# The start of a one-core transformer kernel: smaller first weight pieces, the first norm's squares added by GpSimd, and gates computed one block later

## The reference

```python
def rms_norm(x, g):
    xf = x.astype(jnp.float32)
    y = xf * lax.rsqrt(jnp.mean(xf * xf, axis=-1, keepdims=True) + EPS)
    return (y * g.astype(jnp.float32)).astype(x.dtype)

def even_mix(h, w_in, conv_w, conv_b, ln_g, ln_b, gate_w2, gate_b, gla_norm_g, w_out):
    ...
    p = h @ w_in
    ...
    a_val, a_gate, q, k, v, r, glr = jnp.split(p, cuts, axis=-1)
    y_a = conformer_conv(a_val, a_gate, conv_w, conv_b, ln_g, ln_b)
    log_a = jax.nn.log_sigmoid((glr @ gate_w2 + gate_b).astype(f32)) / GLA_GATE_TAU
    o = gla_chunked(q..., k..., v..., log_a...)
    o = rms_norm(o, gla_norm_g).reshape(B, S, hv).astype(h.dtype)
    y_b = o * jax.nn.silu(r)
    return jnp.concatenate([y_a, y_b], axis=-1) @ w_out

def first_block(x, ...):
    for layer in range(DEPTH):
        h = rms_norm(x, ev_norm_mix[j])
        x = x + even_mix(h, ...)
        h = rms_norm(x, ffn_norm[layer])
        x = x + peer_ffn(h, ...)
```

## Time and profile before

| | us |
|---|---|
| median of 3 runs | 2277.54 (2275.99 to 2280.52) |
| profiled execution | 2274.92, span 2273.1 |
| TensorE busy | 2242.3 (99%) |
| VectorE busy | 1743.5 (77%) |
| ScalarE busy | 1323.0 (58%) |
| GpSimd busy | 586.3 (26%) |

### The profile page before, as it was taken

How to read it: one execution, slowest core, us unless ns; L and a number is a source line. 1 busy time by engine, 2 the same in 40 slices (tenths; PEclk the granted TensorE clock), 3 DMA queues, 4 the chain that set the end, 5 groups by cost and what they waited for, 6 DMA issues and landing times.

```text
span 2273.1 us, 36462 instructions
## 1 busy us (share of the span) xinstructions
PE 2242.3 (99%) x13873; PEld 1964.5 (86%) x13873; DVE 1743.5 (77%) x3559; ACT 1323.0 (58%) x2400; POOL 586.3 (26%) x411
## 2 busy tenths in 40 slices
PE   8999999999999999999999999999999999999999
PEld 8889888888787878888988888888888878899998
DVE  7966999899787878667499998976666666747864
ACT  6765665665545554566566666555554455676643
POOL 4820388774000000011017887700000000003000
PEclk9999999999999999999999999999999999999999
DMA  7724577776788888665257777766666665324441
GB/s 275 254 96 146 187 191 185 173 169 168 267 295 282 292 285 292 256 213 202 93 183 193 190 176 171 169 215 223 216 220 217 216 242 205 130 112 176 185 192 61
DMA packets 168790, 455.24 MB, mean 200 GB/s; under 512 B 44885, under 2 KB 80285, under 8 KB 160681
## 3 DMA queue, kind: packets, MB, share of 16 engines
q1 hardware_dynamic: 135024, 452.40, 58.5%
q0 software_dynamic: 33280, 0.15, 4.1%
q10 hardware_dynamic: 312, 0.37, 0.1%
HBM read 432.76 MB, written 20.09 MB: 199 GB/s over the span
## 4 chain that ended last, share of the span: by engine, by line
PE 85%; DVE 9%; ACT 3%; DMA 2%; issue 1%; ACTq 0%; DVEq 0%
PE PS L174 85%; DVE r_sl L195 3%; DMA mem<-in_v 2%; DVE mem L195 2%; ACT r_sh L185 1%; DVE mem L203 1%; ACT mem L185 1%; DVE mem L209 1%; PE PS L177 0%; DVE hT L203 0%; ACT small L185 0%; DVE mem L215 0%; DMA mem<-in_ada 0%; DMA cst<-in_cst 0%; DVE r_gl L203 0%
## 5 line engine op out<-in xcount | busy, mean ns | idle before, releaser
L195 DVE TENSOR_TENSOR r_sl<-mem,r_sh 128x1024 fp32r<-128x1024 f32 (+2 forms) x750 | 896.3, 1196 | 375.6 <-ACT r_sh L185 374.3
L185 ACT ACTIVATE r_sh<-mem 128x1024 fp32r<-128x1024 f32 (+2 forms) x750 | 768.0, 1025 | 492.5 <-PE PS L174 394.7
L174 PE MATMUL PS<-r_h,r_sh 128*128 128x512 f32 (+2 forms) x3536 | 736.4, 350 | 8.9 <-ACT r_sh L185 4.0
L174 PEld LDWEIGHTS PS<-r_h,r_sh 128*128 128x128 f32 (+1 forms) x3536 | 559.7, 189 | 86.1 <-issue 8.5
L235 POOL DMA_INDIRECT gd<-mem x224 | 407.6, 1820 | 120.1 <-issue 77.5
L174 PEld LDWEIGHTS PS<-r_h,r_sl 128*128 128x128 f32 (+1 forms) x2832 | 381.0, 191 | 23.4 <-DVE r_sl L195 3.6
L174 PE MATMUL PS<-r_h,r_sl 128*128 128x256 f32 (+1 forms) x2832 | 399.7, 283 | 1.2 <-DVE r_sl L195 1.1
L174 PE MATMUL PS<-r_sh,r_ch 128*128 128x512 f32 x1024 | 277.1, 391 | 4.5 <-ACT r_sh L185 2.3
L174 PE MATMUL PS<-r_sh,r_cl 128*128 128x512 f32 x1024 | 274.8, 389 | 0.0
L174 PE MATMUL PS<-r_sl,r_ch 128*128 128x512 f32 x1024 | 274.7, 389 | 0.0
L174 PEld LDWEIGHTS PS<-r_sh,r_ch 128*128 128x128 f32 x1024 | 190.6, 188 | 51.7 <-ACT r_sh L185 7.5
(11 more groups left out here) (177 smaller groups left out, 2548.1 us busy)
## 6 DMA issues: line engine op xcount, KB each, us to landing
mem<-in_u SPq DMA_DIRECT2D x256, 512.0 KB, 3.9
mem<-in_v SPq DMA_DIRECT2D x256, 512.0 KB, 4.4
mem<-in_w SPq DMA_DIRECT2D x16, 2048.0 KB, 7.7
mem<-in_ada SPq DMA_DIRECT2D x48, 512.0 KB, 5.3
mem<-in_in SPq DMA_DIRECT2D x9, 2048.0 KB, 8.8
gd<-cst SPq DMA_DIRECT2D x16, 1024.0 KB, 9.8
mem<-in_wq SPq DMA_DIRECT2D x8, 2048.0 KB, 8.9
r_h<-gd SPq DMA_DIRECT2D x62, 256.0 KB, 4.8
```

Source lines behind the costliest of these rows:

```text
L174: return self.did(self.e and self.e.matmul(out, lhsT, rhs, start=start, stop=stop, skip_group_check=skip))
L185: return self.did(self.e and self.e.activation(out, in_, func, **kw))
L195: return self.did(self.e and self.e.tensor_tensor(out, a, b, op))
```

## The change

The second piece of the first projection's weights (512 columns) becomes three, of 128, 128 and 256 columns; SyncE starts the first four pieces at once, and the pieces behind them take other buffers of the ring. The squares of chunks 4 to 7 are made by VectorE, ahead of its first `gained_lo`; GpSimd adds the eight squares up, and a single product with ones stands between the high and the low matmuls of block 1. The gate products move behind block 2 and `turn_scale` behind block 3; on ScalarE the cuts of blocks 2 and 4 are moved ahead of the norm's scale and of the gates.

```diff
-EV_RANGES = [(2560, 2576), (1024, 1536), (512, 1024), (0, 512), (1536, 2048), (2048, 2560)]
+EV_RANGES = [(2560, 2576), (1024, 1152), (1152, 1280), (1280, 1536), (512, 1024), (0, 512), (1536, 2048), (2048, 2560)]
...
     def even_po(po):
...
-        for c in range(4, 8):
-            po.wait_ge(f"x{c // 2}", 0)
-            po.tensor_tensor(first_squares[:, c, :], xT[:, c, :], xT[:, c, :], MUL).then_inc("sqP", 0, c)
+        for c in range(1, 8):
+            if c == 1:
+                po.wait_ge("sq", 0, 0)
+            else:
+                po.wait_ge("sq_add", 0, c - 1)
+            po.wait_ge("sq" if c < 4 else "sqV", 0, c)
+            po.tensor_tensor(first_squares[:, 0, :], first_squares[:, 0, :], first_squares[:, c, :], ADD).then_inc("sq_add", 0, c)
...
     def even_ac(ac):
...
         hi(ac, 1)
+        hi(ac, 2)
         scale_ac(ac, 0)
...
-        hi(ac, 2)
         hi(ac, 3)
+        hi(ac, 4)
         for c in range(2):
             ac.wait_ge("gate", c)
...
         ac.activation(w1, w1, ACT.Ln, bias=onet).then_inc("softplus", 0)
-        hi(ac, 4)
         turned_scale(ac, 0, 0)
...
     def even_ve(ve):
+        for c in range(4, 8):
+            ve.wait_ge(f"x{c // 2}", 0)
+            ve.tensor_tensor(first_squares[:, c, :], xT[:, c, :], xT[:, c, :], MUL).then_inc("sqV", 0, c)
...
     def even_pe(pe):
-        pe.wait_ge("one", 0)
-        for c in range(4):
-            square_sum(pe, 0, c, first_squares)
...
-        gained_block(pe, 0, 5, (hhiv, hlov), 0, ("scaled_e", 0), (4, 5, 6, 7), first_squares)
+        def first_total(pe):
+            pe.wait_ge("one", 0)
+            square_total(pe, 0, first_squares)
+
+        gained_block(pe, 0, 5, (hhiv, hlov), 0, ("scaled_e", 0), ())
         for n in range(1, 9):
-            block_T(pe, n, n % 8, ("scaled_e", n))
+            if n == 1:
+                bank_wait(pe, 1)
+                mm_T(pe, n, PS[:, 1, 0:256], (hhiv, hlov), between=lambda: first_total(pe))
+                emptied[1] = ("scaled_e", n)
+            else:
+                block_T(pe, n, n % 8, ("scaled_e", n))
+            if n == 3:
+                turn_scale(pe, 0, 0)
             if n == 2:
-                turn_scale(pe, 0, 0)
-            if n == 1:
                 pe.wait_ge("gw2", 0)
                 pe.wait_ge("scaled_e", 0)
...
     def sync(sp):
...
-        load(sp, pieces[0])
-        load(sp, pieces[1])
+        for x in pieces[0:4]:
+            load(sp, x)
...
-        sp.wait_ge(f"w{pieces[1].slot}", pieces[1].g)
-        load(sp, pieces[2])
+        sp.wait_ge(f"w{pieces[3].slot}", pieces[3].g)
+        load(sp, pieces[4])
```

More of the change, by code:

```diff
@@ L109 @@
         ("gla_ac", "uhalf bf softplus lexp decay kdrow meanS ysq varL rstd o osq oln orr silu_r"),
-        ("gla_ve", "usum cumsum ldiff dd level qd kd centred normed yb"),
+        ("gla_ve", "sqV usum cumsum ldiff dd level qd kd centred normed yb"),
         ("gla_pe", "gate lmm kdT kv mean var gla oss"),
@@ L501, in square_sum @@
             pe.wait_ge(*emptied[0])
-        pe.wait_ge("sqP" if k == 0 and c >= 4 else "sq", k, c)
+        pe.wait_ge("sq", k, c)
         last = pe.matmul(PS[:, 0, 0:256], ones, (hT if of is None else of)[:, c, :], c == 0, c == 7)
@@ L658, in take @@
         return arena[:, o - n:o]
-    for p in range(6):
+    for p in range(8):
         piece("ev_in", p)
-        (cut_R if p == 4 else cut_T)("ev_in", p)
+        (cut_R if p == 6 else cut_T)("ev_in", p)
     EV_IN = list(range(len(parts)))
@@ L714, in even_sp @@
     def even_sp(sp):
-        for x in pieces[3:8]:
+        for x in pieces[5:10]:
             load(sp, x)
```

## The result

The changed kernel takes 2285.12 us (median of 7 runs, 2282.91 to 2286.52), the kernel before 2277.54 in the same comparison (7 runs, 2275.02 to 2280.52): ratio 1.0037, 95% interval 1.0027 to 1.0047. It is 7.6 us slower. The prediction was 2281.4 with a range to 2285.1: the sign and the chain were right, the size was half of what came, and the median lies at the very edge, outside.

A forecast was written before the change was run, and what follows sets the result against it. VectorE's row from the gates' softplus was taken to bound block 10. Block 1's start (+0.5 us) and the later gates (+3.4) summed to 3.9 us, added to the median 2277.54: 2281.4 us, range 2277.0 to 2285.1.

The forecast's parts named there:

- The chain of the earlier trace and the 0.56 us: Up to block 10: VectorE's row from the softplus decides; TensorE, waiting 0.56 us for a cut, is only that far ahead.
- rival (a): TensorE's row bounds after all and VectorE's has slack: 2275.4 to 2279.3 us, middle 2277.4; chance 0.14.
- Part 4: Gates a block later: the softplus on VectorE moves from S + 6.95 to S + 10.35, costing 3.4 us.
- V: Mark for VectorE's start on softplus: 21.45 us before, forecast at S + 10.35 after.
- S: Mark for the first matmul of block 1: 14.5 us before, forecast 15.0 after.
- Part 3: Start: VectorE's four squares and contention with GpSimd's seven adds delay the remainders, moving S by +0.5, ends -1.9 and +1.4.
- The end without contention: Start: VectorE at 0.36 to 0.40 us throughout, sixth remainder ending at 11.0, S = 12.6; as a rival 2279.0 us, chance 0.11.
- Part 2: Smaller weight pieces at block 1: its cut ends about 11.9 us instead of 14.1, so the weights stop bounding.
- part 5: Weight buffer ring turned by two: first expert tiles land by 187 us, first read at 197.43, free by 10 us.
- A shift at 44 us should reach the end whole.: Behind 44 us one alternating chain, nothing timed from program start, so block 10's 3.9 us delay stays to the end.
- rival (c): Clock stays low at the start: 2285.1 us if through blocks 0 and 1, halfway 2283; chance 0.25 together with another rival.
- same: Measured time within about 0.2%, 4.6 us, of the kernel before, not to be told from no change; chance 0.62.

The follow-up runs named there:

- gates only: Kernel before with only the gates moved one block later (TensorE's order and ScalarE's cut of block 4 ahead of them): 2281.67 us, ratio 1.0021.
- norm moved back: Kernel before with the smaller weight pieces and the later gates, but its own norm: 2283.31 us, ratio 1.0034.
- pieces only: Kernel before with only the smaller weight pieces and so the turned ring: 2277.06 us, ratio 1.0005.
- VectorE adds: Kernel before with smaller pieces, GpSimd's four squares added up by VectorE, one late product with ones instead of four: 2275.93 us, ratio 0.9993.
- gates only clean: Kernel before with gates one block later, GpSimd's gate scaling held until VectorE made kd, 20 extra matmuls before block 10: 2279.80 us, ratio 1.0013.
- six warming products: Changed kernel with six extra products with ones ahead of block 0, into an unused bank: 2282.95 us, ratio 1.0028.
- four warming products: Changed kernel with four extra products with ones ahead of block 0, into an unused bank: 2283.31 us, ratio 1.0028.
- adds later: Changed kernel with GpSimd's seven adds waiting until VectorE has made its eighth remainder: 2287.83 us, ratio 1.0052.

## Why the prediction was right and wrong

**The chain of the earlier trace rows and the 0.56 us.** Right. VectorE's row from the softplus sets block 10, and rival (a), TensorE's own row, fell: "gates only" leaves TensorE's work and block 1 as they were and costs 6.9 us by 200.

**Part 4, 3.4 us for the gates.** The sum was right: V - S = 10.3 in the changed kernel (10.35 forecast), 7.86 with the gates back, 6.95 before. Only 2.45 of the 3.4 are the gates' place, though; 0.9 come with the later norm's sum and stay when the gates go back. In the kernel before, the move alone is worth 2.9. The cut of block 4 ahead of the gates and a whole block stand where forecast. The wait amid block 4 was 0.97, not 1.35.

**Part 3, S.** The mechanism was right, the size not. I had block 1 at 15.0 with ends 12.6 and 15.9; it came at 15.7, and up to 16.5 in other traces of this start. The term mis-sized is VectorE beside GpSimd, by its price and not by its count: I had five to six meetings at 0.36, 2.0 us; six of the seven adds met VectorE's four squares and first two remainders, which came up to 0.87 apart, where such instructions come 0.33 to 0.40 apart alone. VectorE took 7.75 us from its first square to its eighth remainder, and 5.0 when the adds were held back: 2.7 us. The sixth remainder ended at 13.7 instead of 13.05. The end without contention, S = 12.6, was good: 12.8 when the adds were held back.

**Part 2 and part 5.** Right: no weight wait, -0.09 us by 200 for pieces and ring together.

**"A shift at 44 us should reach the end whole."** This is the step that failed, on both sides of 44 us. Ahead of it I moved VectorE's row as a block, though GpSimd's gate scaling had its own release (ScalarE's sigmoid) and so came to another place in it: 1.3 us. Block 10 came at 50.26, not near 48.3. Behind it I took TensorE's longer wait as mere waiting; the clock fell in it, 1.1 us, and again near 137 us, another 1.1, which came only in traces with the long first fall. With these 2.2 and the 1.3, 3.9 becomes 7.4, and the rest is S. That the time landed where rival (c) had put it (2285.1) is chance. (c)'s first half came: block 0 ran at half clock, 0.21 us a matmul, until 14.5. Its dear half didn't: block 1 ran at 0.12. The slow clock that cost 2.2 us was thirty microseconds further, and I had looked for it only at the start.

**The range.** It ended at rival (c)'s dear end, where the sum's own terms had errors of one sign: every meeting of engines that it left out or priced too low adds. The chances of 0.62 for "same" rested on the 3.9.

## What to carry to other kernels

When a row of one engine is moved in time, look at every other engine that shares something with it, a port or a clock, and ask where their work now falls; the shift isn't the sum of the moved steps alone. A wait that grows from half a microsecond to three on TensorE can cost more than its length, since what follows may run at half clock (2.2 to 2.7 us in four traces, 0.3 to 0.4 in two); 20 extra matmuls in it cost nothing that the trace shows. And before squares or adds are spread over VectorE and GpSimd together, price them as if one engine did them all: beside each other VectorE's squares and remainders came 0.87 us apart instead of 0.33 to 0.40, GpSimd's adds 0.87 instead of 0.80, so a pair took no less than VectorE alone would have needed for both.

## What the hardware showed that I had not expected

- **Who comes first at the shared port.** In the trace before, GpSimd's gate scaling was released at 40.59 amid VectorE's unbroken row. Its first multiplication took 2.55 us and VectorE lost nothing (six in 2.63). In the changed kernel it was released at 43.99, just before the row; the two then took turns, 0.87 us a pair, until GpSimd had done three (2.57 us), and VectorE's six took 3.93. The same instructions cost VectorE nothing or 1.3 us by whether GpSimd comes 0.7 us behind the row's first or 0.5 us ahead of it. The other traces bear it out: GpSimd 0.6 to 0.9 us behind gave six in 2.63 or 2.64 in three more, 0.46 to 0.49 ahead gave 3.91 to 3.93 in six more. The Trainium skill (SBUF — State Buffer, "Who interferes with whom") says that issue order decides who blocks; the traces agree, and add that it decided for the whole row.
- **The clock's rise.** Full clock by 9.0 to 10.6 us in seven traces in which products with ones ran from 6.1 to 6.3 us into block 0 (before, norm moved back, pieces only, gates only, VectorE adds, gates only clean, six warming products); at 14.5, 14.6, 15.5, 15.9 and 16.2 in five, four with a thin start and the one with four warming products and 1.1 us of waiting behind them; with a thin start but the remainders unhindered at 11.5. The moment moves by up to 1.6 us between traces that had the same work until then, so a single trace says little about what a product more or less does. In the stretch tables the granted clock reads 1.00 before its first change although products with ones then stand 0.43 us apart instead of 0.215: ahead of the first change that column can't be trusted, the distance of the starts can.
- **The clock's fall.** TensorE waited 2.98 to 3.00 us before block 10 in six traces. The low clock that followed held for 6.8 us in four of them (the changed kernel, norm moved back, gates only, four warming products) and for 3.4 us in two (adds later, six warming products); a wait of 3.65 us at 15 us and the 1.70 us with GpSimd held back gave 3.4 us too. The clock fell 1.4 us into the wait in the changed kernel (48.7) and in the one of 1.70 (48.8). Waits of 0.30 to 0.97 gave none. The second fall, near 137 us, came in the four traces with the long first one and in no other; with the short one the loss between 40.6 and 200 us was 0.3 to 0.6 us instead of 2.2 to 2.7. What sets the length, and what ties the second fall to the first, is open.
